# A two-block transformer kernel: the first attention woven anew, the second block's first steps reordered, high parts first, and a woven end

## The reference

```python
def first_block(x, ...):
    proj = rms_norm(x, norm_mix_pre) @ w_in
    q, k, v, u, gates = jnp.split(proj, splits, axis=-1)
    y_a = chunk_band_attention(q, k, v, rel_bias) @ w_attn_out
    y_b = multiscale_pool(u, w_pool_group, pool_scale) @ w_pool_out
    g_a, g_b = jnp.split(jax.nn.sigmoid(gates + b_gate), 2, axis=-1)
    x = x + rms_norm((g_a * y_a + g_b * y_b) @ w_o, norm_mix_post)
    return x + rms_norm(conv_gated_ffn(rms_norm(x, norm_ffn_pre), ...), norm_ffn_post)

def second_block(h, p, ...):
    qa, ka, va, qb, kb, vb = jnp.split(rms_norm(h, g_mix) @ w_in, ..., axis=-1)
    oa = diff_attention(qa, ka, va, ...)
    ob = neighbourhood_attention(qb, kb, vb, ...)
    h = h + jnp.concatenate([oa, ob], axis=-1) @ w_out
    h = h + hier_moe(rms_norm(h, g_ffn), w_rg, w_re, w1, w3, w2)
    return h + rms_norm(p @ w_ple, g_ple) * jax.nn.sigmoid(rms_norm(h, g_plg) @ w_plg)
```

## Time and profile before

| | us |
|---|---|
| median of 3 runs | 1639.23 |
| lowest, highest | 1638.41, 1641.41 |
| profiled execution | 1641.76 |
| its span in the trace | 1639.7 |
| mean granted clock of TensorE | 0.985 of full |

### The profile page before, as it was taken

The page is one execution under the profiler, slowest core; times in us unless marked ns, Lnnn a source line. Parts: engine busy times, 40 slices in busy tenths (PEclk is TensorE's granted clock), DMA queues, the critical chain, the costliest instruction groups (busy, mean ns, idle before and its releaser), DMA issues. The chain is left out here.

```text
span 1639.7 us, 20000 instructions
## 1 busy us (share of the span) xinstructions
PE 1569.1 (96%) x7970; PEld 1105.5 (67%) x7970; DVE 724.5 (44%) x1228; ACT 532.8 (32%) x910; POOL 161.8 (10%) x170
## 2 busy tenths in 40 slices
PE   6999899999999999999999899999999999999969
PEld 5776588789888888887777777744444444444459
DVE  5334422445544444468565777521122222212364
ACT  5233422334433323344454667321100110110052
POOL 1012200101201111111300210010000000000000
PEclk9999999999999999999999989999999999999979
DMA  6111232222322222222110222749999999999921
GB/s 264 54 50 59 106 113 103 92 76 96 123 80 75 107 100 103 103 90 86 44 52 27 103 103 78 295 184 386 421 420 420 421 418 421 421 417 421 415 93 53
DMA packets 46158, 307.05 MB, mean 187 GB/s; under 512 B 5216, under 2 KB 7520, under 8 KB 10992
## 3 DMA queue, kind: packets, MB, share of 16 engines
q1 hardware_dynamic: 43344, 296.22, 45.6%
q0 software_dynamic: 2720, 9.52, 1.6%
HBM read 301.52 MB, written 4.19 MB: 186 GB/s over the span
## 5 line engine op out<-in xcount | busy, mean ns | idle before, releaser
L590 DVE TENSOR_TENSOR w_lo<-M,w_hi 128x2048 fp32r<-128x2048 f32 x73 | 169.2, 2323 | 192.8 <-ACT w_hi L585 192.8
L2379 PE MATMUL bank<-M 128*64 128x512 f32 x1024 | 229.1, 599 | 3.8 <-DMA M<-in_w 3.7
L585 ACT ACTIVATE w_hi<-M 128x2048 fp32r<-128x2048 f32 x73 | 139.0, 1910 | 163.6 <-PE bank L762 62.3
L762 PE MATMUL bank<-HTH,w_hi 128*128 128x512 f32 x432 | 168.1, 389 | 0.0
L762 PE MATMUL bank<-HTL,w_hi 128*128 128x512 f32 x432 | 168.1, 389 | 0.0
L762 PE MATMUL bank<-HTH,w_lo 128*128 128x512 f32 x432 | 168.0, 389 | 0.0
L2379 PEld LDWEIGHTS bank<-M 128*64 128x64 f32 x1024 | 71.6, 137 | 140.8 <-issue 139.8
L2396 PE MATMUL bank<-M 128*64 128x512 f32 x512 | 114.0, 596 | 1.9 <-DMA M<-in_w 1.9
L2510 DVE TENSOR_TENSOR X<-bank,X 128x512 f32<-128x512 f32 x72 | 48.1, 688 | 115.8 <-PE bank L2412 115.7
L762 PEld LDWEIGHTS bank<-HTL,w_hi 128*128 128x128 f32 x432 | 81.1, 188 | 16.9
L762 PEld LDWEIGHTS bank<-HTH,w_hi 128*128 128x128 f32 x432 | 81.1, 188 | 16.8
(11 more groups left out here) (338 smaller groups left out, 3014.7 us busy)
## 6 DMA issues: line engine op xcount, KB each, us to landing
M<-in_w SPq DMA_DIRECT2D x192, 1024.0 KB, 10.1
M<-in_wd SPq DMA_DIRECT2D x78, 1024.0 KB, 4.8
M<-in_nb SPq DMA_DIRECT2D x4, 1536.0 KB, 6.5
M<-in_rows POOLq DMA_DIRECT2D x5, 512.0 KB, 4.1
X<-in_x SPq DMA_DIRECT2D x4, 512.0 KB, 9.0
M<-in_tb POOLq DMA_DIRECT2D x8, 256.0 KB, 4.0
ple_raw<-M POOLq DMA_DIRECT2D x4, 512.0 KB, 2.9
M<-ple_raw SPq DMA_DIRECT2D x4, 512.0 KB, 6.9
```

Of the source, the lines that this page charges most:

```text
L585: e.activation(hi[:, :], slots[slot_of[n]], ACT.Copy).then_inc(split_hi_done, 1)
L590: e.tensor_tensor(lo[:, :], slots[slot_of[n]], hi[:, :], ALU.subtract).then_inc(split_lo_done, 1)
L762: m = e.matmul(out[:, :], w[:, k0 + k, n0:n0 + 128], v[k], start=(k == 0 and i == 0), stop=(k == len(hi) - 1 and i == 2))
L2379: m = e.matmul(b[64 * s:64 * s + 64, :], Xe[:, 4 * kh + k, o + C * s:o + C * s + C], unit_w(key, 4)[:, k, :], start=(kh == 0 and k == 0), ...
```

## The change

**First block.** q and k of head pair 3 are woven at steps 18 to 21 (16 to 19 before), u(1) at 16, 17 (20, 21), and in4's buffers are given up at step 18 (21). Banks of the attention are now fixed: scores 2 or 3, woven products 0 or 1, transposes 5 or 7, outputs 4 or 6. Nine of the 12 matmuls of the attention's half of y(0, 0) and y(0, 1) (k = 0, 1, 2) come at steps 33 and 34, the last three of each after the attention (`y_pe`, which multiplies for the given k alone).

**Second block, first steps.** Token tiles 0 and 1 take the high part of in2 1 first and its low part after, with tile 3's transposes behind them; the tiles 2 and 3 as before. In the neighbourhood attention the copies of the values are shared out anew: ACT copies 4, 5, 6 at step 0, behind o_a's high part; DVE copies 2 at step 0 and 3, 7 at step 2; the low parts of o_a come at step 2, behind the scores. out2 0 and out2 2 are multiplied high part first (`gemm_rows_part`, as `gemm_tok_part` below, for one k range).

**Experts.** The last three pieces of scatter 7 stand behind down 15; the last half of down 15 finishes bank h = 0 before h = 1. Of the embedding product, ACT now sums the squares as it copies the banks, and DVE multiplies the rows by the gain, before they go to HBM; the end loses both. POOL writes rows 0, 1 behind the first one_hot. Before the experts POOL also writes the normed input's two parts XSH and XSL to HBM (xs_d, 2 x 2.1 MB), where the overflow path would fetch them from.

**The end.** It is in the same block as the experts; the overflow check comes behind the output, and with a count above 0 the end would be done again (`again`). The list END weaves: norm's transposes "n", high parts of the weights by HTH "a" and by HTL "b", low parts by HTH "c0", "c1" (units plg 0, 1). Units are halves of 512 columns; each gate tile is 512 columns wide (24 matmuls), the last one in two of 256. The four splits have PH buffers of their own, and PL lies in the slots. The square root's table is loaded after the last Silu. Output pieces are 256 KB, the last two 128 KB.

```diff
-        for hp, at in ((1, (4, 5, 6, 7)), (2, (8, 9, 10, 12)), (3, (16, 17, 18, 19))):
+        for hp, at in ((1, (4, 5, 6, 7)), (2, (8, 9, 10, 12)), (3, (18, 19, 20, 21))):
...
-        for g, at in enumerate(((13, 14), (20, 21), (22, 23), (24, 25))):
+        for g, at in enumerate(((13, 14), (16, 17), (22, 23), (24, 25))):
...
+        Y_FIRST = {33: 0, 34: 1}
...
-        VJ_FIRST, VJ_ACT = (0, 1), (4, 6)
+        VJ_FIRST, VJ_ACT, VJ_DVE = (0, 1), {0: (4, 5, 6)}, {0: (2,), 2: (3, 7)}
...
-        turns = itertools.cycle((5, 1, 2, 0, 3, 4))
-        NBR_BANKS = {"vj": (4, 0, 3, 6, 4, 0, 5, 3), "oa": {2: 7, 3: 4}, 1: (1, 2), 2: (1, 2), "nt": (0, 3)}
+        turns = itertools.cycle((0, 5, 4, 1, 2, 3))
+        NBR_BANKS = {"vj": (4, 0, 3, 6, 4, 0, 5, 3), "oa": {2: 7, 3: 4}, "ns": (1, 2), "nt": ((0, 5), (3, 7))}
...
-        MOE += scatter(6, 5, 6, 7) + scatter(7, *range(8)) + steps_of(NPAIR, 2) + scatter(8, *range(8))
+        MOE += scatter(6, 5, 6, 7) + scatter(7, *range(5)) + steps_of(NPAIR, 2) + scatter(7, *range(5, 8)) + scatter(8, *range(8))
...
+        END = [("n", 0), ("n", 1), ("a", 0), ("b", 0), ("n", 2), ("a", 1), ("b", 1), ("c0", 0), ("c0", 1), ("a", 2), ("c1", 0), ("c1", 1),
+               ("n", 3), ("b", 2), ("c0", 2), ("c1", 2), ("a", 3), ("b", 3), ("c0", 3), ("c1", 3)]
+        OUT = [(n, t, 0, 512) for n in range(2) for t in range(TT)][:-1] + [(1, 3, 0, 256), (1, 3, 256, 256)]
...
+        def gemm_tok_part(e, key, j, t, out, low):
+            w = list(parts(key, 4))[low]
+            for k in range(4):
+                for i, src in enumerate((HTH,) if low else (HTH, HTL)):
+                    m = e.matmul(out[:, :], src[:, 4 * j + k, t * 128:(t + 1) * 128], w[:, k, :],
+                                 start=(j == low == k == i == 0), stop=(j == 1 and low == 1 and k == 3))
+            return m
...
+        def high_ready(e, key):
+            e.wait_ge(split_hi_done, split_index(unit[key]) + 1)
...
-        A_SPLIT = {4: ("in", 1), 6: ("in", 2), 8: ("in", 3), 21: ("in", 4), 22: ("in", 5), 24: ("in", 6), 27: ("in", 7)}
+        A_SPLIT = {4: ("in", 1), 6: ("in", 2), 8: ("in", 3), 18: ("in", 4), 22: ("in", 5), 24: ("in", 6), 27: ("in", 7)}
...
+                if i in Y_FIRST:
+                    for g in range(3):
+                        taken(e, ("ao", g))
+                    split_ready(e, ("ap", 0))
+                    y_pe(e, Y_FIRST[i], claim(e, ("y", 0, 0, Y_FIRST[i]))[0], range(3))
...
-                        gemm3_T(e, ("ap", i), 128 * j, *claim(e, ("y", i, q, j)), *y, k0=4 * q)
+                        if i == q == 0:
+                            y_pe(e, j, bank[ps.at["y", 0, 0, j][0]], [3]).then_inc(fills_of(("y", 0, 0, j)), 1)
+                        else:
+                            gemm3_T(e, ("ap", i), 128 * j, *claim(e, ("y", i, q, j)), *y, k0=4 * q)
...
+                    if (t0, j) == (0, 1):
+                        high_ready(e, ("in2", 1))
+                        for t in (0, 1):
+                            gemm_tok_part(e, ("in2", 1), 1, t, bs[t][0], 0)
+                        split_ready(e, ("in2", 1))
+                        for t in (0, 1):
+                            gemm_tok_part(e, ("in2", 1), 1, t, bs[t][0], 1).then_inc(bs[t][1], 1)
+                        norm_pe(e, 2, 3)
...
+                    high_ready(e, ("out2", 2 * h))
+                    gemm_rows_part(e, ("out2", 2 * h), t, b, 0)
                     split_ready(e, ("out2", 2 * h))
-                    gemm3_rows(e, ("out2", 2 * h), 0, t, b).then_inc(fills, 1)
...
                     nbr_exp_act(e, i)
-                for v in VJ_AT.get(i, ()):
-                    if v in VJ_ACT:
-                        evac_act(e, Vj[:, v, :], ("vj", v))
                 if i in OA_AT:
                     oa_hi_act(e, OA_AT[i])
+                for v in VJ_ACT.get(i, ()):
+                    evac_act(e, Vj[:, v, :], ("vj", v))
...
                     nbr_score_dve(e, i)
+                for v in VJ_DVE.get(i, ()):
+                    evac_dve(e, Vj[:, v, :], ("vj", v))
+                if i == 2:
+                    oa_lo_dve(e, OA_AT[0])
...
-                for v in VJ_AT.get(i, ()):
-                    if v not in VJ_FIRST + VJ_ACT:
-                        evac_dve(e, Vj[:, v, :], ("vj", v))
-                if i in OA_AT:
-                    oa_lo_dve(e, OA_AT[i])
+                if i == 2:
+                    oa_lo_dve(e, OA_AT[2])
                 if i - 1 in O2_SPLIT:
...
-            load_gain(e, 4)
+            o = BIG["ple"]
+            e.dma_start(rowb[:, :], rows_d[:, o:o + D].to_broadcast([128, D])).then_inc(d_rowb, 16)
+            for i, x in enumerate((XSH, XSL)):
+                e.dma_start(xs_d[i], x[:, :, :].bitcast(F32)).then_inc(d_xs, 16)
...
+            for k, h in [(0, 0), (1, 0), (0, 1), (1, 1)] if (p, kh) == (NPAIR - 1, 1) else [(0, 0), (0, 1), (1, 0), (1, 1)]:
...
+            act_own.mark(e.activation(junk[:, 0, 0:512], b[:, :], ACT.Square, accum_out=PL_ST[0][:, at:at + 1]))
...
+        def ple_dve(e, t):
+            e.wait_ge(d_rowb, 48)
             for h in range(2):
                 taken(e, ("pl", t, h))
+            e.tensor_tensor(STAGE[t], STAGE[t], rowb[:, :], ALU.mult).then_inc(pl_row, 1)
+            if t == 3:
...
                 if what == "down" and at[1] == 1:
                     p = at[0]
...
+        def end_pe(e):
+            first, second = range(4), range(4, 8)
+            for what, t in END:
+                if what == "n":
+                    norm_pe(e, 4, t)
+                    continue
+                out, fills = bank[ps.at["pg", 0, t, 0][0]], fills_of(("pg", 0, t, 0))
+                if what == "a":
+                    claim(e, ("pg", 0, t, 0))
+                    e.wait_ge(n_hi, 2 * (NORM_N[4] + t) + 2)
+                    for j, ks in enumerate((first, second)):
+                        gate_hi(e, j)
+                        gate_part(e, out[:, :], 0, t, ks, HTH, 0, start=(j == 0))
+                if what == "b":
+                    ht_ready(e, 4, t)
+                    gate_part(e, out[:, :], 0, t, range(KD), HTL, 0)
+                if what == "c0":
+                    split_ready(e, ("plg", 0))
+                    gate_part(e, out[:, :], 0, t, first, HTH, 1)
+                if what == "c1":
+                    split_ready(e, ("plg", 1))
+                    gate_part(e, out[:, :], 0, t, second, HTH, 1, stop=True).then_inc(fills, 1)
+            split_ready(e, ("plg", 3))
+            for n, t, o, w in OUT[TT:]:
+                b, fills = claim(e, ("pg", n, t, o))
...
+        def end_act(e):
+            e.wait_ge(d_xs, 32)
+            for j in range(2):
+                split_act(e, unit["plg", j])
+            norm_act(e, 4, 0, 0)
+            norm_act(e, 4, 1, 0)
+            norm_act(e, 4, 0, 3)
+            norm_act(e, 4, 2, 0)
+            norm_act(e, 4, 1, 3)
+            norm_act(e, 4, 2, 3)
+            norm_act(e, 4, 3, 0)
+            split_act(e, unit["plg", 2])
+            embed_root_act(e)
+            norm_act(e, 4, 3, 3)
+            split_act(e, unit["plg", 3])
...
+        def end_dve(e):
+            def sums(t):
+                for h in range(2):
+                    scatter_dve(e, 8, t, h)
+            sums(0)
+            sums(1)
+            norm_dve(e, 4, 0, 1)
+            norm_dve(e, 4, 1, 1)
+            sums(2)
+            norm_dve(e, 4, 0, 4)
+            norm_dve(e, 4, 2, 1)
+            norm_dve(e, 4, 1, 4)
+            split_dve(e, unit["plg", 0])
+            sums(3)
+            split_dve(e, unit["plg", 1])
+            norm_dve(e, 4, 3, 1)
+            norm_dve(e, 4, 2, 4)
+            split_dve(e, unit["plg", 2])
+            norm_dve(e, 4, 3, 4)
+            ss, sq, r = PL_ST
```

More of the change, by code:

```diff
@@ L2474, in moe_dve @@
                         rounds_dve(e)
+                        for t in range(2):
+                            ple_dve(e, t)
+                if what == "pl" and at[1] == 1:
+                    ple_dve(e, at[0])
                 if what == "gs":
@@ L2847, in overflow @@
             clear(o_own)
+        again()
 def _by_cols(w, width=256):
```

375 lines of the change are left out of this document (228 added, 147 removed).

## The result

The changed kernel takes **1612.91 us** (median of 4 runs, 1609.41 to 1615.84), the kernel before in the same call 1638.82 us: a ratio of 0.984, with a 95% interval of 0.9815 to 0.9864. It is 1.6% faster. The forecast was 1607 us, 32 us less; 26 us came.

A forecast was written before the change was run, and what follows sets the result against it. TensorE, busy for 96% of the span, was taken as the bound. Terms of -4.0, -2.5, -2.6, -7, -16 and 0 sum to -32.1 us: 1609.7, as a median 1607 us; ends 1598 and 1619, range 1599 to 1619 at .8.

The forecast's parts named there:

- Term 1: Mid-attention, first block: an earlier split removes PE's 3.27 us low-part wait and its slow clock; -4.0 us (-3 to -4.5).
- Term 2: Attention's tail: y matmuls moved into steps 33 and 34, new banks remove a 2.2 us wait; -2.5 us (-1 to -4.8).
- Term 3: Second block's in-projection: high part first removes a 2.73 us wait, tile 3 gets a new 1.8 us one; -2.6 us.
- Term 4: Neighbourhood attention's start: waits of 2.06, .98, 2.61 us and slow clock go, new 2.4 us wait; -7 us (-3 to -9.5).
- Term 5: Experts' end to output: last scatter 1.6 us earlier, norms woven into wider gates, overflow check moved; -16 us (-12 to -18).
- the gates' part: End: gates start at about 1572 instead of 1588.40, 192 matmuls of 512 columns, last ends at 1619.5; -16.6 us.
- the tail: Behind the last gate matmul: order stays, the overflow branch runs while the store lands; up to .7 us, .6 taken.
- Term 6: Before the experts: the new 4.19 MB write to HBM fits in 23 us of free DMA time; 0, worst case 10 us.
- One sign: Experts: the prediction is wrong if PE's waits for the experts' weights (M<-in_w) grow by over 2 us.
- The rival that only the end gains: The four early places swap their waits for bank waits, 4 of 16 us remain: -20, 1619 to 1620 us; chance .12.
- The write's rival: Before the experts: the new HBM write delays the weight loads by the full 10 us: 1617 us; chance .10.
- The slow-clock rival: At the end, PE's stop-and-go around the norms keeps all gates at the low clock: 39 us lost, 1646 us; chance .04.

The follow-up runs named there:

- e5: The changed kernel with the first block as before (its weave, its banks, y behind the attention): 1620.16 us.
- e6: The changed kernel with all 24 matmuls of y(0,0), y(0,1) for the attention's half behind the attention again, weave and fixed banks kept: 1611.98 us.
- e8: The changed kernel, but PE waits for both parts of in2 1 before tokens 0 and 1, high part still first: 1613.51 us.
- e10: The changed kernel with tile 3's in-projection transposes behind tile 2's 12 products with in2 0 instead of ahead: 1613.07 us, ratio .9816.
- e7: The changed kernel with the neighbourhood attention's value copies, low parts and banks as before, high part first kept: 1614.54 us.
- e9: The changed kernel, but PE waits for both parts of out2 0 and out2 2 before each of their products: 1611.42 us.
- e0: The changed kernel run once more, nothing edited: 1612.27 us.
- e4: The changed kernel, but at the end PE does all four tiles' norm transposes first, then each tile's gates: 1622.33 us.
- e2: The changed kernel without again(), the second run of the end in the overflow path: 1608.25 us.
- e3: The changed kernel without the whole overflow path, its register load and branch: 1608.64 us.
- e1: The changed kernel without the write of the normed input's two parts to HBM and ACT's wait for it: 1613.20 us.

## Why the prediction was right, and where its sizes were off

The direction, the range and the order of the terms were right; the time came out 6 us above the forecast, by these steps.

- **Term 1 (-4.0)** measured -4.2: the low-part wait and its slow matmuls went. e5 gives terms 1 and 2 back together, 6.9 us.
- **Term 2 (-2.5)** measured -2.4, but for the wrong reason. I had let .98 us of idle time hide some of the moved matmuls, and then took .7 off for ACT. In fact none of the 4.1 us was hidden (the .98 us are there still) and nothing was lost: the bank's 2.2 us is all but the whole term (e6). That forecast and measurement meet is luck, an error of 1.0 us against one of .7.
- **Term 3 (-2.6)** measured -2.65, with the new wait of 1.8 us that I had worked out (1.79). It is shown by e8; e10 shows that it is a chain's, not the order's.
- **Term 4 (-7)** measured -6.0. The new wait was forecast at 2.4 and is 2.57, in the place and for the copy named. The size was off by the clock: I had counted the slow matmuls there as gone, and behind the new wait they are back in seven of the ten profiles, for 1.0 us. In the three without them the stage is 7.0 us shorter than before, the forecast itself. The first product of out2(0,0) was to come some 7 us earlier and came 4.5 us earlier (22.2 us behind the difference attention's event instead of 26.7), 6.2 at full clock. e7 and e9 show that either half of the change alone gives 4 to 5 us, so the waits that I had added up one by one overlap.
- **Term 5 (-16)**: the gates' part was forecast at -15.0 (56.5 us from the last scatter to the last matmul) and measured -15.9, to -17.4 in e0. e4 shows that 12 us of it are the weave. Of the 1.6 us ahead of the last scatter the wait did go (1.78 to .20 us). That the stretch got shorter by it is not shown: it took 508.1 us where the kernel before took 508.0, and 506.3 on the mean over the eleven others, but its spread is 3 us and the kernel before has one profile. **The step that failed is the tail: "the branch, which runs while the store lands, may cost up to .7 us; I take .6".** It costs 3.1 us. I had taken it from the check's place before, where PE's branch is .36 us long; the change had also doubled the code behind it, and I priced that at nothing since it does not run. e2 and e3 show it. This is the one miss that every run has, 2.5 of the 6 us.
- **Term 6 (0)** holds as far as e1 can tell, and for the reason given: the DMA engines had room. One sign stood on its line: PE's waits for the experts' weights were not to grow by over 2 us and grew by 2.0 (5.6 to 7.6), but without the write they are 7.2.
- *Chance.* The slow matmuls at 374 (1.5 us), the later start (.8 us) and the long weights' stretch (1.8 us above the mean of the others) of this one profile are not the change's. They fall out of the medians in part: the profile is 2.9 us above its median, as the one before was 2.5 above its own.

The rival that only the end gains has nothing for it: the four early places gave 15.2 of the 16.1 us forecast, and e5 shows that such gains pass. The write's rival falls with e1. The slow-clock rival had a small grain: from the last scatter to the last gate matmul it takes 54.1 us in four profiles and 55.2 to 55.8 in the others that have this stage unedited, so 1 to 1.7 us, never the stage.

## What to carry to other kernels

Code that never runs has a price where it is jumped over: here doubling the untaken path added 3.5 to 3.9 us to PE's branch, at a place where nothing covers it. Of two remedies for the waits of one place, price the second with the first already in; the sum of the two is too much. And matmuls that were moved ahead of a copy on which the rest waits gained nothing here: they pushed the copy back by what they took. Last, when two profiles of a stage are a microsecond apart, compare the granted clock in both before the edit is given the credit.

## What the runs showed that I had not expected

PE's branch took .36 and .40 us over some 218 of its instructions, and 3.9 to 4.25 us over some 413 in all eleven profiles that have it; ACT's, POOL's and DVE's, over shorter code, 45 to 72 ns. A shorter form of the second end, which would keep the overflow path whole and might win e2's 4 us, was not run, and how long the jump may be stays open between the two lengths.

Where a slow stretch of PE's clock falls differs from run to run of one kernel: behind the transposes at 374 in one profile of the changed kernel, and at 186 in the other, with nothing different ahead of either. It makes 1 to 1.6 us each, where the smallest term measured 2.4.
